# Start of a hybrid decoder step: where VectorE waits for its table of constants, and the order of the first high and low parts

## The reference

```python
def rms_norm(x, g):
    xf = x.astype(jnp.float32)
    y = xf * lax.rsqrt(jnp.mean(xf * xf, axis=-1, keepdims=True) + RMS_EPS)
    return (y * g.astype(jnp.float32)).astype(x.dtype)
...
    h = rms_norm(x, lw['attn_norm'])
    proj = h @ lw['w_in']
```

## Time and profile before

| what | value |
|---|---|
| median of 3 runs | 904.88 us (904.15 to 908.27) |
| the profiled execution | 907.78 us |
| its span, first to last instruction | 906.1 us |
| TensorE busy | 881.9 us, 97% of the span |
| VectorE, ScalarE busy | 639.3 us (71%), 450.2 us (50%) |

### The profile page before, as it was taken

How to read it: one execution, slowest core, us unless ns; L and a number is a source line. 1 busy time by engine, 2 the same in 40 slices (tenths; PEclk the granted TensorE clock), 3 DMA queues, 4 the chain that set the end, 5 groups by cost and what they waited for, 6 DMA issues and landing times.

```text
span 906.1 us, 21269 instructions
## 1 busy us (share of the span) xinstructions
PE 881.9 (97%) x8588; PEld 768.6 (85%) x8588; DVE 639.3 (71%) x1083; ACT 450.2 (50%) x771; POOL 61.9 (7%) x95
## 2 busy tenths in 40 slices
PE   5999999999999999999899999999999999999998
PEld 4999899998998787877556899977998899889986
DVE  5564277656665974886824753799879887988796
ACT  6432545412332388886525425544674467436741
POOL 0000111213510000000000001010100000000000
PEclk9999999999999999999999999999999999999999
DMA  8443687853220569679987336787788433444343
GB/s 278 154 134 109 146 180 207 246 106 92 77 62 3 196 219 363 227 242 339 364 333 276 101 94 172 200 242 216 211 225 270 140 118 114 146 138 121 109 145 145
DMA packets 73163, 164.47 MB, mean 182 GB/s; under 512 B 5918, under 2 KB 32126, under 8 KB 70890
## 3 DMA queue, kind: packets, MB, share of 16 engines
q1 hardware_dynamic: 59370, 124.26, 39.8%
q0 software_dynamic: 13696, 38.85, 18.1%
HBM read 156.55 MB, written 40.10 MB: 217 GB/s over the span
## 4 chain that ended last, share of the span: by engine, by line
PE 85%; DVE 7%; DMA 4%; ACT 2%; issue 2%; SPq 0%; DVEq 0%; ACTq 0%; POOLq 0%
PE PS L982 16%; PE PS L984 16%; PE PS L983 16%; PE PS L1174 8%; PE PS L1337 5%; PE PS L1359 3%; PE PS L1409 2%; PE PS L1015 2%; PE PS L1297 2%; PE PS L1445 2%; PE PS L1323 2%; DVE WL L2916 1%; PE PS L1314 1%; PE PS L1643 1%; PE PS L1642 1%
## 5 line engine op out<-in xcount | busy, mean ns | idle before, releaser
L983 PE MATMUL PS<-WL,U 128*128 128x512 f32 x224 | 87.6, 391 | 0.0
L982 PE MATMUL PS<-WH,U 128*128 128x512 f32 x224 | 87.5, 391 | 0.0
L2037 ACT ACTIVATE WH<-Wraw 128x1024 fp32r<-128x1024 f32 x56 | 57.8, 1054 | 51.7 <-DMA Wraw<-tau 21.2
L2916 DVE TENSOR_TENSOR WL<-Wraw,WH 128x1024 fp32r<-128x1024 f32 x56 | 66.8, 1218 | 7.3 <-ACT WH L2037 7.3
L1174 PE MATMUL PS<-AR 64*64 64x64 f32 x1912 | 61.2, 220 | 3.4 <-issue 1.6
L982 PE MATMUL PS<-WR,HR 128*128 128x384 f32 (+1 forms) x184 | 63.8, 347 | 0.8 <-issue 0.8
L1174 PEld LDWEIGHTS PS<-AR 64*64 64x64 f32 x1912 | 58.7, 135 | 6.0 <-issue 3.9
L982 PE MATMUL PS<-h2H,WH 128*128 128x288 f32 x208 | 61.5, 296 | 1.2 <-DVE rc L3038 1.2
L983 PE MATMUL PS<-h2L,WH 128*128 128x288 f32 x208 | 61.3, 295 | 0.0
L984 PE MATMUL PS<-h2H,WL 128*128 128x288 f32 x208 | 61.2, 294 | 0.0
L984 PE MATMUL PS<-WH,U 128*128 128x512 f32 x152 | 59.2, 390 | 0.0
(11 more groups left out here) (436 smaller groups left out, 2305.0 us busy)
## 6 DMA issues: line engine op xcount, KB each, us to landing
AR<-in_cache_kv SPq DMA_DIRECT2D x120, 384.0 KB, 5.0
tau<-in_w_mlp_down POOLq DMA_DIRECT2D x24, 1024.0 KB, 9.2
Wraw<-tau SPq DMA_DIRECT2D x16, 1024.0 KB, 4.8
Wraw<-in_w_mlp_up SPq DMA_DIRECT2D x14, 1024.0 KB, 5.6
Wraw<-in_w_mlp_down SPq DMA_DIRECT2D x12, 1024.0 KB, 5.1
W<-in_w_in SPq DMA_DIRECT2D x6, 1536.0 KB, 9.0
QK<-in_cache_kv SPq DMA_DIRECT2D x8, 384.0 KB, 5.6
AR<-in_x_prompt SPq DMA_DIRECT2D x4, 512.0 KB, 9.1
```

Of the source, the lines that this page charges most:

```text
L982: mm(out, lH, rH, start=start, stop=False, skip_group_check=skip)
L983: mm(out, lH, rL, start=False, stop=False, skip_group_check=skip)
L2037: f(piece_half(WH, r, d, h), piece_half(Wraw, r, d, h), ACT.Copy).then_inc(w_hi, 1)
L2916: tt(piece_half(WL, r, d, h), piece_half(Wraw, r, d, h), piece_half(WH, r, d, h).bitcast(F32), SUB).then_inc(w_lo, 1)
```

## The change

VectorE's wait for `prm` moves from ahead of scale_input(0) to behind it, that is, to just ahead of take_turned(0). On ScalarE split_rows(0) goes ahead of first_high(0). On VectorE rows_low(0) goes ahead of first_low(0), and take_turned(1), which stood between the two, now stands behind first_low(1). Everything else is unchanged.

```diff
@@ ScalarE @@
             row_deviation(0)
             row_deviation(1)
+            split_rows(0)
             first_high(0)
-            split_rows(0)
             first_high(1)
             first_high(2)
             split_rows(1)
@@ VectorE @@
+            scale_input(0)
             dve.wait_ge(in_prm, 16)
-            scale_input(0)
             take_turned(0)
             scale_input(1)
+            rows_low(0)
             first_low(0)
-            rows_low(0)
+            first_low(1)
             take_turned(1)
-            first_low(1)
             scale_input(2)
             first_low(2)
             rows_low(1)
```

## The result

The changed kernel took 910.51 us (median of 18 runs, 907.94 to 913.72), the kernel before 906.67 us (18 runs, 903.96 to 910.22). The ratio is 1.0048 (95% interval 1.0036 to 1.0060): slower by about 4 us, just under the half per cent named in the prediction, five times the 0.71 forecast and above the upper end of the range. The profiled execution took 908.89 us.

What follows compares the result with a forecast made beforehand. TensorE, busy 97% of the span, was taken as the bound, gated by the third group's low part. -1.29 + 0.65 + 0.09 + 1.26 = +0.71 us on the median 904.88 gave 905.6 us, range 903.5 to 909.0.

Steps and rivals of the forecast that it cites:

- Edit one, "1.29 us earlier": VectorE's wait for the table moved behind scale_input(0): tile 0's reciprocal starts at 5.81 instead of 7.10, 1.29 us earlier.
- The order on VectorE: first_low(1) now ahead of take_turned(1) on VectorE: adds 1.26 us to the second tile's turned rows.
- The loss of 0.65: VectorE's second reciprocal waits until 10.68 for ScalarE's root, which hangs on tile 1's transfer: 0.65 us of gain lost.
- the gate: TensorE's last two products of the first tile, needing the third low part: forecast to move from 20.23 to 20.94.
- The bound of the prediction for an early tile 1, +0.27: If tile 1 lands 0.65 us or more earlier, the sum is -1.29 + 0.30 + 1.26 = +0.27 us.
- rival D: TensorE's clock falls to half in the longer pause before the first tile's last two products: 908.5 us, chance 0.08.
- 2.7 at most: TensorE's pause before the first tile's last two products: at most 1.32 + 0.7 + 0.71 = 2.7 us.
- The bound of 0.7: TensorE's 22 first-tile products that need no third low part start and end at most 0.7 us earlier.
- The price of the stretch: If TensorE's clock falls for 5.8 us, as at the start, half is lost: +2.9 us on top of 0.7.
- Rival C: One of TensorE's three later waits for transfers swallows the 0.71 us, giving 904.9 us; chance 0.15.
- rows 2: Profile rows of TensorE's waits after 21 us: three end on a transfer, 1.5, 1.0 and 0.2 us long.
- Rival B: The 1.29 us gained at the table's wait is kept to the end, giving 903.6 us; chance 0.05.

Runs made afterwards that it cites:

- the second trace of before: The kernel before, unchanged, traced once more: the table landed 4.0 us after its issue, and TensorE's pause before the first tile's last two products was 1.33 us.
- the changed kernel with its pause filled: Changed kernel plus six keep_busy products, read by nothing, on TensorE ahead of its wait for the third low part; ratio to before 1.0006, median 908.16 us.
- the run with 2.17: Changed kernel with take_turned(1) back ahead of first_low(1); TensorE's pause 2.17 us; ratio to before 1.0002, median 908.36 us.
- the reordered version: Changed kernel with take_turned(1) ahead of first_low(1), first_low(2) ahead of scale_input(2), row_deviation(2) ahead of split_rows(1); ratios to before 0.9986 and 0.9985, medians 906.35 and 905.41 us.

## Why the prediction was wrong

**The base.** Of the 4.9 us between the forecast 905.6 and 910.51, 1.8 belong to the kernel before: the median of three runs, 904.88, was put under the sum, and that of 18 is 906.67. With 904.88 as the kernel before, the change as measured would have given 908.7, inside the range. The other 3.1 are the change itself, +3.8 where +0.71 was forecast, and they are what the rest explains.

**Edit one, "1.29 us earlier": the term of the sum that failed.** The forecast start of the first reciprocal, 5.81, was right (5.76). The row that it was taken from was not: 7.10 belongs to an execution whose table landed 5.3 us after its issue, and in the traces since it was 3.6 to 4.0. With the table landing so, the move is worth 0.08 us. The prediction bounded one landing, that of tile 1, and took the table's own as fixed, though the whole gain hung on it.

**The order on VectorE: right.** take_turned(1) was to lose 1.26 behind first_low(1), and it did: from 13.43 to 15.01 is 1.58, which is 1.26 for first_low(1), about 0.35 for rows_low(0), which now waits for ScalarE's high part (11.26, where VectorE would have been free near 10.9), and -0.04 for the earlier start, which add up to it within 0.01 (the wait for the high part was put at 0.09, or 0.30 with an early tile 1). The loss of 0.65 by tile 1's landing did not occur, since the tile landed by 7.6. With the 1.29 gone as well, the sum is 1.58 instead of 0.71, and the gate moved by as much, 20.59 - 19.02 = 1.57. The bound of the prediction for an early tile 1, +0.27, lacks the 1.25 us that the table was not late, and 0.05 of the wait for the high part.

**The clock, rival D at 0.08: the step that failed.** The mechanism and its form were in the text, but its chance was far too low. Two judgements went wrong. The pause was put at 2.7 at most, as 1.32 + 0.7 + 0.71, and was 3.86: against the second trace of before the first products start 0.96 us earlier (12.61 against 13.57) and the gate comes 1.57 later, and 1.33 + 0.96 + 1.57 = 3.86. So 0.86 of the excess is the gain that the wait did not bring. The bound of 0.7 hung on tile 1's landing at 9.17, which the prediction let vary in its sum but not here: with the tile there by 7.61, its turns ran at 11.05 and not 11.6. TensorE's timeline in the changed kernel, then in the second trace of before:

```profile
11.05 1.10 PE L975 MATMUL PS<-cst,AR 128*128 128x128 f32 x8 [0.54 <-DVE AR L2236]
...
12.61 0.44 PE L1028 MATMUL PS<-WR,HR 128*128 128x384 f32 x1
...
13.57 0.44 PE L1028 MATMUL PS<-WR,HR 128*128 128x384 f32 x1 [0.53 <-DVE rcL L2253]
```

And 2.7 was called nearer the harmless end of 1.32; the run with 2.17 lost the clock in its trace. The price of the stretch was guessed too high, 2.9 us, as half of a stretch of 5.8: in the first trace the clock was low from about 21.1 to 24.5, 3.4 us (worked out from the windows), and the mark is 3.20 behind before, of which 1.57 is lateness and 1.6 the clock, about half of that stretch. In the second trace the mark is 4.08 behind with 1.59 of lateness (20.61 against 19.02), so 2.5 is the clock: there it fell near 19.2, ahead of the gate, and rose near 26.0. Lateness and clock together, 3.2 to 4.1 at the mark, agree with 3.5 to 3.8 between the medians on the same chips.

Of the two things that the prediction weighed, the row of before, a granted clock of 1.00 from 10 to 12 us while the turns ran at half the pace, was the misleading one. The other was the rule of the Trainium skill's page TensorE: Matmul & The Clock Gate (Part 1: The HAM clock gate) that the half rate is the default and activity lifts it. With that the trace after agrees: granted clock 0.50 behind the pause, 1.00 once TensorE had been busy again.

**Rival C, that a later wait swallows the shift: not borne out.** The medians are 3.8 and 3.5 us apart, where the mark was 3.2 and 4.1 late, and the single traces say the same (a span of 903.0 us in the second trace of before, 907.2 and 906.7 in the changed kernel). The waits that this rival hung on differ between executions: of the 1.5 and 1.0 us in rows 2 the second trace of before has 0.2 and 0.5. Two further entries of the full list, 1.6 and 0.8 us, end on nothing that the profile shows, and not on another engine's work, as the prediction read them all. **Rival B**, that the gain passes, fell with the gain itself.

## What to carry to other kernels

A gain that is one transfer's wait should be taken from more than one execution's landing: here all but 0.08 us of it was the scatter of a 28 KB transfer. And when part of TensorE's work is pulled ahead without its last gate moving, look at the pause that this opens: it can cost as much in TensorE's clock as the order costs by itself, or more (here 1.6 and 2.5 us against 1.6). Products that nothing reads won the clock's part back here; the gate's own work moved forward won back both parts at the mark.

## What the runs showed that was not expected

A pause of 2.17 us was enough for the clock to fall in one trace, while pauses of 1.3 kept it in four (the two of before, that with the wait alone, and that of the changed kernel with its pause filled). The length of the pause alone does not settle it: ahead of the output products the first trace of before paused for 1.50 us at 451.61 and kept the clock, and the first trace of the reordered version paused for 1.64 and lost it. The second trace of the reordered version lost it at two places in the recurrence, near 235 and 256 us. Nor does the fall come at a fixed time after the pause begins: in the first trace of the changed kernel it came half a us after TensorE had resumed (21.1 against 20.59), in the second 1.4 us before it did. TensorE's timeline in the first trace of the reordered version:

```profile
451.10 5.35 PE L1445 MATMUL PS<-rc,HM 128*128 128x512 f32 x8 [1.64 <-DMA rc<-in_w_out]
```

and the window behind that pause:

```profile
451.00:455.00 4.00, 3.90 (x6) 0.57 1.03 399
```

So the clock can fall now at one of these pauses and now at another, and the spread between runs of one kernel goes along with it: of the two sets of 23 runs of before, the five with a mean clock of 0.998 or less have medians of 910.05 and 910.65 us, the other 18 of 905.96 and 905.93. That the falls are the whole of this difference is not shown.
